# Moving the layer-norm gain rows from VectorE to GpSimd in a fused encoder layer, with two small steps of ScalarE and VectorE put in another place

## The chip, the cores and the metric

The kernel runs on one core of one Trainium2 chip. Its time is the device time in microseconds (us). Engines are named PE (TensorE), ACT (ScalarE), DVE (VectorE), POOL (GpSimd) and SP (the engine that issues most DMAs).

## The reference, cut to what matters

One encoder layer over two sequences (512 and 1024 rows of width 1024, 12 tiles of 128 rows in all). After a token mixer (stage one) and before a mixture of experts (stage three), this is computed per row:

```python
mod = silu(c) @ w_ada + b_ada            # one row per sequence: sh1, sc1, g1, sh2, sc2, g2
mix = token_mixer(...) @ w_out           # [A|B] W_out
x = layer_norm(ALPHA * x + g1 * mix, ln1_g, ln1_b)
h = x * (1 + sc2) + sh2                  # goes to the router and to the experts
logits = h @ [w_route_group | w_route_expert]
```

The kernel folds the modulation of h into the norm. With `rstd` and the negative mean `m` of a row's residual r, `h = (r + m) * G * rstd + B`, where `G = (1 + sc2) * ln1_g` and `B = sh2 + (1 + sc2) * ln1_b`. G and B depend on the sequence q alone (q = 0 for tiles 0 to 3, q = 1 for tiles 4 to 11), and are kept as 128x1024 rows, the same in every partition. Here they are called the gain rows.

## The kernel before, in words

Each engine has its own instruction list, written by hand; engines meet at semaphores alone, and an engine never passes a wait. The stage that the change touches follows stage one (the token mixer over six pairs of tiles) and runs once over the 12 tiles t. Every fp32 product with weights is done as three matmuls on a high and a low part (`three`).

PE, for each tile t from 2 on: `mix_half(t, 0)` (24 matmuls of 512 columns), then `route(t - 2)` (the router's 8 products; in tile 2 it is `h2_transposes(0)` instead), every second tile a small `rank` or `pick`, then `mix_half(t, 1)` (24 more), in tile 2 also `route(0)`, then `h2_transposes(t - 1)`. Its waits: `route(t)` waits for `h2T_copied` (ACT has copied tile t's transposes to SBUF) and for `logit_read` (DVE has taken the logits of tile t - 1 out of the one bank that they share); `mix_half(t, 0)` waits for DVE's low part of z (`z2_l_made`) and for the residual of tile t - 2.

DVE, for each tile: `second(t)` (gate the mix by g1, two reads of PSUM; add ALPHA x; the mean), `low_z(t + 2)`, `h2_out(t)` (the variance, then two SCALAR_TENSOR_TENSOR instructions: (r + m) * G, and * rstd + B), `x1_out(t)` (the same two with ln1_g and ln1_b), `logits_out(t - 1)`, and then `select` (even tiles: the top experts) or `places` and `picks` (odd tiles). `h2_out(t)` writes a single buffer h2, so that it waits until PE has transposed the tile before.

ACT, for each tile: `high_z(t + 2)`, which waits until PE has made the whole mix of tile t, `copy_h2T(t - 1)`, and `square(t)`, from which DVE's variance comes. In tile 2 `copy_h2T(0)` stands ahead of `high_z(4)`.

POOL does `rstd_of(t)` for each tile, one power of one column, and nothing else in this stage. It hands rstd back to `h2_out(t)`.

The gain rows are made in place by DVE, three instructions of 128x1024 for each q: `gain_first(q)` (two) and `gain_last(q)` (one). For q = 0 the first two stand ahead of stage one's last steps `gate_u(5)` and `b_out(5)`, the third behind them. For q = 1 all three stand between tiles 1 and 2. Both wait for `mod2_loaded`, DMAs that SP issues: ln1_g, ln1_b, g1, sc2, sh2 for q = 0 (80 in all), and three more for q = 1 (128).

After the stage PE, DVE and POOL finish the lists of rows for each expert, and the experts' loop (stage three) runs to the last stage.

Of the kernel before, what the change touches and what calls it, by code (L numbers as in the profile page):

```python
# [26 lines left out]
ALU = mybir.AluOpType  # L27
# [8 lines left out]
SEQ_TILES = ((0, SEQS[0] // P), (SEQS[0] // P, NT))  # L36
# [73 lines left out]
def encoder(nc, ins, outs):  # L110
    ctx = ExitStack()
    with ctx:
# [129 lines left out]
        sc2b = r.take("sc2b", [P, D])  # L242
        sh2b = Region(PB0).take("sh2b", [P, D])
# [8 lines left out]
        g1b, sc2b, sh2b = [[halves(b), w_col[:, 2 * j + 2:2 * j + 4, 1, :]] for j, b in enumerate((g1b, sc2b, sh2b))]  # L252
        ln_g2, ln_b2 = halves(ln_g), halves(ln_b)
        gain_tmp, squares1 = w_mid[:, 4:6, 1, :], w_mid[:, 6:8, 1, :]
# [108 lines left out]
        def bcast(row, n):  # L363
# [10 lines left out]
        S = {n: sem(n) for n in (  # L374

            "c_loaded rows_loaded small_loaded sp_rows_loaded wsp_loaded ident_made c_silu cT_made c_ready c_low mod_init"
            " colsT_made cols_ready wspT_made wspT_ready rowsum_made rowsum_ready off_made off_ready"
            " edge_iota spl_ones"

            " x_loaded xT_made x0_ready ada_h_made ada_l_made ada_made mod_hl_made mod_cols mod_made"  # L380
            " k_mod k_high k_low win_h_made win_l_made h_ready hT_h_made hT_l_made"
            " late_h_made late_l_made late_made late_row added_h added_l g2_loaded g2_made g2_row g2_added"
# [5 lines left out]
            " res_ready var_ready rstd_ready shift_ready x1_ready x1_stored h2_ready h2_stored h2T_made h2T_copied"  # L388
            " logit_made logit_read"

            " rt_consts sel_ready ranked rank_read pick_ready picked tab_ready eid_ready list_pe list_dve w_act"

            " idx_ready gathered xgT_made xT_h_made xT_l_made gu_split_h gu_split_l dn_split_h"
            " dn_split_l gu_used dn_used silu_made act_ready aT_e_made aT_h_made aT_l_made y_ready"
# [264 lines left out]
        def _(pool):  # L659
# [60 lines left out]
            def rstd_of(t):  # L720
                pool.wait_ge(S["var_ready"], t + 1)
                nc.gpsimd.tensor_tensor(rstd[:], mv[:, 1:2], half_neg[:], ALU.pow).then_inc(S["rstd_ready"], 1)  # L722

            for t in range(NT):
                rstd_of(t)

            pool.wait_ge(S["tab_ready"], 1)
            pool.wait_ge(S["h2_stored"], 16 * NT)
# [50 lines left out]
        def _(act):  # L779
# [160 lines left out]
            def copy_h2T(t):  # L940

                act.wait_ge(S["h2T_made"], t + 1)
                if t >= 1:
                    act.wait_ge(S["logit_made"], t)
                for b in range(2):
                    last = nc.scalar.activation(h2T[:, 4 * b:4 * b + 4, :], ps[4 + b][:].rearrange("p (k m) -> p k m", k=4), ACT.Copy)
                last.then_inc(S["h2T_copied"], 1)

            for t in range(NT):
                if t == NT - 4:  # L950
                    act.wait_ge(S["a_ready"], NP)
                    act.wait_ge(S["b_copied"], NP)
                    act.wait_ge(S["fb_copied"], 2)
                if t == 2:
                    copy_h2T(0)
                if t < NT - 2:
                    high_z(t + 2, t % 2, t // 2 + 1)
                if t >= 2:
                    copy_h2T(t - 1)
                square(t)  # L960
            copy_h2T(NT - 1)
# [112 lines left out]
        def _(dve):  # L1074
            st = Steps(dve, S["dve_steps"], S["dve_carrier"])
            nv = nc.vector
# [212 lines left out]
                norm_v(2 * i)  # L1289
            low_wout(1)  # L1290
            norm_v(NT - 1)

            def gain_first(q):

                dve.wait_ge(S["mod2_loaded"], 16 * (5 + 3 * q))
                st.done(nv.scalar_tensor_tensor(gain_tmp, sc2b[q], 1.0, ln_b2, ALU.add, ALU.mult))
                st.done(nv.scalar_tensor_tensor(sc2b[q], sc2b[q], 1.0, ln_g2, ALU.add, ALU.mult))
                st.sync()

            def gain_last(q):  # L1300
                st.done(nv.tensor_tensor(sh2b[q], sh2b[q], gain_tmp, ALU.add))
                st.sync()

            gain_first(0)
            gate_u(NP - 1)
            b_out(NP - 1)
            gain_last(0)

            def second(t, q):

                dve.wait_ge(S["mix_made"], t + 1)
                if t >= 2:
                    dve.wait_ge(S["x1_stored"], 16 * (t - 1))
                for b in range(2):
                    st.done(nv.tensor_tensor(res[t % 2][:, b, :], ps[2 * (t % 2) + b][:], g1b[q][:, b, :], ALU.mult))
                st.sync()
                dve.wait_ge(S["xr_loaded"], 16 * (t + 1))
                nv.scalar_tensor_tensor(res[t % 2], halves(xr), ALPHA, res[t % 2], ALU.mult, ALU.add, accum_out=stat[:, 0:1]).then_inc(S["res_ready"], 1)
                dve.wait_ge(S["res_ready"], t + 1)
                nv.tensor_scalar(mv[:, 0:1], stat[:, 0:1], -1.0 / D, None, ALU.mult).then_inc(S["shift_ready"], 1)  # L1320

            def h2_out(t, q):
                dve.wait_ge(S["res_normed"], t + 1)
                nv.tensor_scalar(mv[:, 1:2], stat[:, 1:2], 1.0 / D, EPS, ALU.mult, ALU.add).then_inc(S["var_ready"], 1)
                dve.wait_ge(S["shift_ready"], t + 1)
                if t >= 1:
                    dve.wait_ge(S["h2_stored"], 16 * t)
                    dve.wait_ge(S["h2T_made"], t)
                st.done(nv.scalar_tensor_tensor(halves(h2), res[t % 2], mv[:, 0:1], sc2b[q], ALU.add, ALU.mult))
                dve.wait_ge(S["rstd_ready"], t + 1)  # L1330
                st.sync()
                nv.scalar_tensor_tensor(halves(h2), halves(h2), rstd[:, 0:1], sh2b[q], ALU.mult, ALU.add).then_inc(S["h2_ready"], 1)  # L1332
# [6 lines left out]
            def logits_out(t):  # L1339
                dve.wait_ge(S["logit_made"], t + 1)  # L1340
                nv.tensor_tensor(logits[:, t, :], ps[6][:, 0:NG + NE], router_b[:], ALU.add).then_inc(S["logit_read"], 1)
# [53 lines left out]
                                         ALU.is_equal, ALU.mult).then_inc(S["pick_ready"], 1)  # L1395

            dve.wait_ge(S["a_ready"], NP)

            for t in range(NT):
                q = 0 if t < SEQ_TILES[0][1] else 1  # L1400
                second(t, q)
                if t == 2:
                    logits_out(0)
                if t < NT - 2:
                    low_z(t + 2, t % 2, t // 2 + 1)
                else:
                    if t == NT - 1:
                        places(4)
                if t == 0:
                    edge_out(NP - 1, 6, 2)  # L1410
                    dve.wait_ge(S["rt_consts"], 10)
                h2_out(t, q)
                if t == NT - 1:
                    picks(4)
                x1_out(t)
                if t == 1:
                    gain_first(1)
                    gain_last(1)
                if t >= 2:
                    logits_out(t - 1)  # L1420
                    if t % 2 == 0:
                        select(t // 2 - 1)
                    elif t < NT - 1:
                        places((t - 3) // 2)
                        picks((t - 3) // 2)
# [546 lines left out]
```

## Time and profile before

| | us |
|---|---|
| median of 3 runs | 1327.22 (1326.94 to 1330.86) |
| time of the profiled execution | 1326.94 |
| its span in the profile | 1325.2 |
| busy: PE, DVE, ACT, POOL | 1225.8, 951.3, 643.6, 198.8 |
| mean granted TensorE clock | 0.967 of full speed |

The span is what lies between the first and the last instruction; the run's own time is 1.7 us longer. Times of day below ("at 359.82") count from the span's start. The stage in question lies between about 341 and 505 us. Matmuls are pipelined, so that a matmul record may begin before the one ahead of it has ended.

### The profile page before, as it was taken

The page shows a single profiled execution, that of the slowest core. Times are in us where ns is not written, and L with a number is a line of the kernel's source. Part 1 is how long each engine was busy: PE and PEld are TensorE (multiplying, and loading weights), DVE is VectorE, ACT ScalarE, POOL GpSimd, SP SyncE. Part 2 cuts the span into 40 slices and gives each one's busy share as a digit, 9 for nine tenths or more (in the row PEclk, how much of TensorE's full clock was granted, in tenths as well). Part 3 has the DMA queues.
Part 4 walks back from the last instruction along what each step waited for, and adds up shares of the span by engine and source line. Part 5 has one row for each costly group of instructions (what it writes and reads, how often), then busy time and mean ns, then how long its engine had stood idle before and what let it go on. Part 6 is the DMA issues. An engine that isn't in the chain of part 4 may idle for free.

```text
span 1325.2 us, 23169 instructions
## 1 busy us (share of the span) xinstructions
PE 1225.8 (93%) x6396; PEld 1009.1 (76%) x6397; DVE 951.3 (72%) x1203; ACT 643.6 (49%) x666; POOL 198.8 (15%) x242
## 2 busy tenths in 40 slices
PE   4989989999999997799999999999999999999490
PEld 4778879998888872688888888888888888888240
DVE  3666555457899987854788656664889988886197
ACT  4453321123221213564677545644777788775221
POOL 0001101000011011111122111111121222212022
PEclk8899989999999998899999999999999999999796
DMA  9743231015432457775999757775999999996983
GB/s 309 240 126 105 88 96 49 17 30 193 160 112 112 175 211 281 271 266 212 360 384 401 299 221 299 261 269 205 366 400 398 390 407 389 398 395 224 384 303 127
DMA packets 121645, 329.08 MB, mean 248 GB/s; under 512 B 12040, under 2 KB 43904, under 8 KB 121604
## 3 DMA queue, kind: packets, MB, share of 16 engines
q1 hardware_dynamic: 107412, 288.08, 58.4%
q0 software_dynamic: 12320, 34.15, 7.3%
q10 hardware_dynamic: 1872, 6.29, 1.2%
q8 instruction: 26, 0.43, 0.1%
q14 instruction: 15, 0.12, 0.0%
HBM read 296.97 MB, written 39.42 MB: 254 GB/s over the span
## 4 chain that ended last, share of the span: by engine, by line
PE 72%; DVE 17%; DMA 3%; issue 3%; ACT 2%; POOL 1%; SPq 0%; DVEq 0%; POOLq 0%; ACTq 0%
PE bank L1582 17%; PE bank L1584 17%; PE bank L1583 17%; PE bank L1595 3%; PE bank L1597 3%; PE bank L1596 3%; PE bank L1878 3%; POOL rstd L722 1%; PE bank L1902 1%; DVE h L1332 1%; DMA y_rows<-y_sb,s_idx 1%; DVE gu_l L1467 1%; DVE fin L1546 1%; DVE fin L1561 1%; DVE gated L1542 1%
## 5 line engine op out<-in xcount | busy, mean ns | idle before, releaser
L1467 DVE TENSOR_TENSOR gu_l<-gu_raw,gu_h (+1 forms) x128 | 287.3, 2285 | 40.7 <-ACT gu_h L966 26.9
L1582 PE MATMUL bank<-gu_h,xT_h 128*128 (+1 forms) x624 | 248.6, 398 | 6.3 <-DVE xT_l L1486 3.7
L1584 PE MATMUL bank<-gu_h,xT_l 128*128 (+1 forms) x624 | 244.7, 392 | 0.0
L966 ACT ACTIVATE gu_h<-gu_raw (+1 forms) x128 | 238.7, 1928 | 11.8 <-issue 11.6
L1583 PE MATMUL bank<-gu_l,xT_h 128*128 (+1 forms) x624 | 244.3, 392 | 0.0
L1471 DVE TENSOR_TENSOR dn_l<-dn_raw,dn_h (+1 forms) x64 | 143.6, 2285 | 5.9 <-issue 4.2
L1582 PEld LDWEIGHTS bank<-gu_h,xT_h 128*128 128x128 f32 x624 | 118.3, 190 | 30.3 <-DVE xT_l L1486 4.1
L1584 PEld LDWEIGHTS bank<-gu_h,xT_l 128*128 128x128 f32 x624 | 118.1, 189 | 25.3
L1583 PEld LDWEIGHTS bank<-gu_l,xT_h 128*128 128x128 f32 x624 | 118.5, 190 | 23.5
L1582 PE MATMUL bank<-dn_h,aT_h 128*128 (+1 forms) x312 | 124.8, 400 | 2.5 <-DVE aT_l L1481 2.5
L1584 PE MATMUL bank<-dn_h,aT_l 128*128 (+1 forms) x312 | 121.7, 390 | 0.0
L1583 PE MATMUL bank<-dn_l,aT_h 128*128 (+1 forms) x312 | 121.6, 390 | 0.0
L970 ACT ACTIVATE dn_h<-dn_raw (+1 forms) x64 | 119.1, 1914 | 1.7 <-DMA dn_raw<-in_w_down 1.6
L1595 PE MATMUL bank<-hT_h,win_h 128*128 128x256 f32 x384 | 111.3, 290 | 8.6 <-ACT z2T L865 4.4
L976 ACT ACTIVATE act_s<-bank 128x512 f32<-128x512 f32 x39 | 23.3, 598 | 182.9 <-PE bank L1584 182.9
L1597 PE MATMUL bank<-hT_h,win_l 128*128 128x256 f32 x384 | 108.9, 284 | 0.0
L1596 PE MATMUL bank<-hT_l,win_h 128*128 128x256 f32 x384 | 108.8, 283 | 0.0
L751 POOL DMA_INDIRECT y_rows<-y_sb,s_idx x39 | 72.1, 1849 | 194.1 <-ACT y_sb L996 194.1
L1477 DVE TENSOR_TENSOR act_a<-bank,act_s 128x512 f32<-128x512 f32 x39 | 27.0, 691 | 85.9 <-ACT act_s L976 85.9
L1595 PEld LDWEIGHTS bank<-hT_h,win_h 128*128 128x128 f32 x384 | 74.2, 193 | 11.1 <-DVE hT_l L1127 5.5
L1582 PE MATMUL bank<-wout_h,z_h 128*128 128x512 f32 x192 | 77.4, 403 | 0.0
L1584 PE MATMUL bank<-wout_h,z_l 128*128 128x512 f32 x192 | 75.9, 395 | 0.0
(275 smaller groups left out, 2118.1 us busy)
## 6 DMA issues: line engine op xcount, KB each, us to landing
gu_raw<-in_w_gate_up SPq DMA_DIRECT2D x128, 1024.0 KB, 7.6
dn_raw<-in_w_down SPq DMA_DIRECT2D x64, 1024.0 KB, 7.4
y<-y_rows SPq DMA_DIRECT2D x24, 512.0 KB, 5.0
ada_raw<-in_w_ada SPq DMA_DIRECT2D x20, 512.0 KB, 5.3
ada_raw<-in_w_ada SPq DMA_DIRECT2D x10, 1024.0 KB, 5.3
win_raw<-in_w_in SPq DMA_DIRECT2D x8, 768.0 KB, 7.5
h_rows<-h SPq DMA_DIRECT2D x12, 512.0 KB, 2.6
fin<-x_rows SPq DMA_DIRECT2D x12, 512.0 KB, 13.9
```

The source lines that it names most:

```text
L751: nc.gpsimd.indirect_dma_start(out=y_d, out_offset=bass.IndirectOffsetOnAxis(ap=s_idx[:, 0:1], axis=0), in_=y_sb[:], in_offset=None, bound ...
L966: nc.scalar.activation(gu_slot(gu_h, e, c), gu_slot(gu_raw, e, c), ACT.Copy).then_inc(S["gu_split_h"], 1)
L970: nc.scalar.activation(dn_slot(dn_h, e, c), dn_slot(dn_raw, e, c), ACT.Copy).then_inc(S["dn_split_h"], 1)
L1467: nv.tensor_tensor(gu_slot(gu_l, e, c), gu_slot(gu_raw, e, c), gu_slot(gu_h, e, c).bitcast(F32), ALU.subtract).then_inc(S["gu_split_l"], 1)
L1471: nv.tensor_tensor(dn_slot(dn_l, e, c), dn_slot(dn_raw, e, c), dn_slot(dn_h, e, c).bitcast(F32), ALU.subtract).then_inc(S["dn_split_l"], 1)
L1582: mm(out, lh, rh, start=start, stop=False)
L1583: mm(out, lh, rl, start=False, stop=False)
L1584: return mm(out, ll, rh, start=False, stop=stop)
L1595: mm(out, win_h[:, k, c], hT_h[s][:, k, :], start=start, stop=False)
L1596: mm(out, win_h[:, k, c], hT_l[s][:, k, :], start=False, stop=False)
L1597: return mm(out, win_l[:, k, c], hT_h[s][:, k, :], start=False, stop=stop)
L1878: last = nc.tensor.transpose(ps[2 + k // 4][:, (k % 4) * P:(k % 4 + 1) * P], xg[:, k * P:(k + 1) * P], ident[:])
```

## The change

Five edits, all around the gain rows:

1. POOL gets `gain_rows(q, part)`. Part 0 waits for `mod2_loaded`, makes sc2 + 1 in place and multiplies it by ln1_b into `gain_tmp`; part 1 adds `gain_tmp` to sh2 in place and multiplies sc2 + 1 by ln1_g in place. These are four instructions of 128x1024 for each q, where DVE had three. A new semaphore `gains_made` counts the finished q.
2. For q = 0 both parts stand ahead of POOL's first `rstd_of`; for q = 1 part 0 follows `rstd_of(1)` and part 1 follows `rstd_of(2)`.
3. DVE loses `gain_first` and `gain_last`. It waits for `gains_made` in each `h2_out`, and for `mod2_loaded` before the loop and again before tile 4.
4. ACT: in tile 2 `copy_h2T(0)` moves behind `high_z(4)`.
5. DVE: in tile 2 `logits_out(0)` moves from behind `second(2)` to behind `x1_out(2)`.

```diff
+            def gain_rows(q, part):
+                if part == 0:
+                    pool.wait_ge(S["mod2_loaded"], 16 * (5 + 3 * q))
+                    st.done(nc.gpsimd.tensor_scalar(sc2b[q], sc2b[q], 1.0, None, ALU.add))
+                    st.sync()
+                    st.done(nc.gpsimd.tensor_tensor(gain_tmp, sc2b[q], ln_b2, ALU.mult))
+                    st.sync()
+                else:
+                    st.done(nc.gpsimd.tensor_tensor(sh2b[q], sh2b[q], gain_tmp, ALU.add))
+                    nc.gpsimd.tensor_tensor(sc2b[q], sc2b[q], ln_g2, ALU.mult).then_inc(S["gains_made"], 1)
+                    st.sync()
+            gain_rows(0, 0)
+            gain_rows(0, 1)
             for t in range(NT):
                 rstd_of(t)
+                if t in (1, 2):
+                    gain_rows(1, t - 1)
...
-                if t == 2:
-                    copy_h2T(0)
                 if t < NT - 2:
                     high_z(t + 2, t % 2, t // 2 + 1)
                 if t >= 2:
+                    if t == 2:
+                        copy_h2T(0)
                     copy_h2T(t - 1)
                 square(t)
...
-            def gain_first(q):
-                dve.wait_ge(S["mod2_loaded"], 16 * (5 + 3 * q))
-                st.done(nv.scalar_tensor_tensor(gain_tmp, sc2b[q], 1.0, ln_b2, ALU.add, ALU.mult))
-                st.done(nv.scalar_tensor_tensor(sc2b[q], sc2b[q], 1.0, ln_g2, ALU.add, ALU.mult))
-                st.sync()
-            def gain_last(q):
-                st.done(nv.tensor_tensor(sh2b[q], sh2b[q], gain_tmp, ALU.add))
-                st.sync()
-            gain_first(0)
             gate_u(NP - 1)
             b_out(NP - 1)
-            gain_last(0)
...
                 dve.wait_ge(S["shift_ready"], t + 1)
+                dve.wait_ge(S["gains_made"], q + 1)
...
             dve.wait_ge(S["a_ready"], NP)
+            dve.wait_ge(S["mod2_loaded"], 16 * 5)
             for t in range(NT):
+                if t == SEQ_TILES[0][1]:
+                    dve.wait_ge(S["mod2_loaded"], 16 * 8)
                 second(t, q)
-                if t == 2:
-                    logits_out(0)
...
                 x1_out(t)
-                if t == 1:
-                    gain_first(1)
-                    gain_last(1)
                 if t >= 2:
+                    if t == 2:
+                        logits_out(0)
                     logits_out(t - 1)
```

## Rows read from the trace of the kernel before

**Rows 1.** Windows, stage 341 to 505: us, busy of PE, PEld, DVE, ACT, POOL, clock, DMA, GB/s.
```profile
341.00:505.00 164.00, 160.86 (x840) 131.84 (x839) 149.23 (x329) 38.83 (x59) 18.83 (x12) 1.00 0.44 162
```

**Rows 2.** Timeline of PE without the mix: start, us, line; waits in brackets.
```profile
353.36 1.03 PE L1775 MATMUL bank<-ident,h 128*128 128x128 f32 x8
...
359.82 1.87 PE L1797 MATMUL bank<-router_w,h2T 128*128 128x36 f32 x16
361.52 1.07 PE L1775 MATMUL bank<-ident,h 128*128 128x128 f32 x8
...
368.04 1.87 PE L1797 MATMUL bank<-router_w,h2T 128*128 128x36 f32 x16
...
490.78 1.03 PE L1775 MATMUL bank<-ident,h 128*128 128x128 f32 x8
```

**Rows 3.** Waits between 333 and 505: PE's longest, in total, times, longest.
```profile
PE bank L1797 <- DVE logits L1341: 2.0, 1, 2.0
```

**Rows 4.** Timeline of DVE: gain rows, tile 2, and the start of tile 11.
```profile
333.05 1.22 DVE L1296 SCALAR_TENSOR_TENSOR w_mid<-sc2b,ln_b 128x1024 f32<-128x1024 f32 x1 [7.35 <-DMA sh2b<-mod_rows]
...
360.10 1.22 DVE L1296 SCALAR_TENSOR_TENSOR w_mid<-w_col,ln_b 128x1024 f32<-128x1024 f32 x1
...
366.41 0.18 DVE L1341 TENSOR_TENSOR logits<-bank,router_b 128x36 f32<-128x36 f32 x1
...
367.80 0.15 DVE L1324 TENSOR_SCALAR mv<-stat 128x1 f32<-128x1 f32 x1
...
373.37 0.19 DVE L1341 TENSOR_TENSOR logits<-bank,router_b 128x36 f32<-128x36 f32 x1
...
492.04 1.29 DVE L1315 TENSOR_TENSOR res<-bank,w_col 128x512 f32<-128x512 f32 x2
```

**Rows 5.** Timeline of ACT, tiles 1 and 2.
```profile
354.43 1.09 ACT L946 ACTIVATE h2T<-bank 128x512 f32<-128x512 f32 x2
360.02 1.06 ACT L881 ACTIVATE z_h<-z2T 128x1024 fp32r<-128x1024 f32 x1 [4.50 <-PE bank L1584]
362.63 1.09 ACT L946 ACTIVATE h2T<-bank 128x512 f32<-128x512 f32 x2 [1.55 <-PE bank L1775]
366.53 1.15 ACT L938 ACTIVATE w_mid<-w_col,mv 128x1024 f32<-128x1024 f32 x1 [2.81 <-DVE mv L1320]
```

**Rows 6.** Timeline of POOL: a power alone and beside DVE, a copy beside DVE.
```profile
324.57 0.55 POOL L674 TENSOR_TENSOR v_rstd<-v_mv,half_neg 128x1 f32<-128x1 f32 x1 [6.21 <-DVE v_mv L1187]
...
354.78 1.57 POOL L722 TENSOR_TENSOR rstd<-mv,half_neg 128x1 f32<-128x1 f32 x1 [8.04 <-DVE mv L1324]
...
544.63 1.22 POOL L738 COPY g_idx<-table_g 128x1 int32 x1 [15.00 <-PE bank L1878]
```

**Rows 7.** Timeline of DVE beside those POOL instructions.
```profile
354.65 1.28 DVE L1329 SCALAR_TENSOR_TENSOR h<-res,mv,sc2b 128x1024 f32<-128x1024 f32 x1
...
541.32 6.69 DVE L1467 TENSOR_TENSOR gu_l<-gu_raw,gu_h  x3
```

**Rows 8.** Timeline of POOL: instructions of more than one column.
```profile
304.08 0.29 POOL L696 TENSOR_SCALAR_AFFINE_SELECT tri<-tri 128x128 f32<-128x128 f32 x1
304.35 0.44 POOL L701 IOTA iota_c<- 128x384 f32 x1
304.75 0.13 POOL L701 IOTA iota_p<- 128x1 f32 x1
```

**Rows 9.** Timeline of PE where it had been idle, start of the experts' loop.
```profile
548.66 1.12 PE L1902 MATMUL bank<-ident,act_a 128*128 128x128 f32 x4 [4.82 <-DVE act_a L1477]
552.31 0.79 PE L1582 MATMUL bank<-gu_h,xT_h 128*128 x1 [2.54 <-DVE gu_l L1467]
```

**Rows 10.** Windows of PE around them: us, busy, granted clock, DMA, GB/s.
```profile
548.00:550.00 2.00, 1.12 (x4) 0.67 0.29 37
550.00:552.00 2.00, 0.00 (x0) 0.50 0.62 229
...
554.00:556.00 2.00, 2.00 (x7) 0.63 0.00 0
```

More of the change, by code:

```diff
@@ L389, in encoder @@
             " logit_made logit_read"
-            " rt_consts sel_ready ranked rank_read pick_ready picked tab_ready eid_ready list_pe list_dve w_act"
+            " gains_made rt_consts sel_ready ranked rank_read pick_ready picked tab_ready eid_ready list_pe list_dve w_act"
             " idx_ready gathered xgT_made xT_h_made xT_l_made gu_split_h gu_split_l dn_split_h"
```

## The prediction

> **What bounds the kernel now.** I read the windows by stage first. Between 341 and 505 us PE is busy 160.86 of 164 us and DVE 149.23 [rows 1], so the busy shares alone leave it open which of the two sets the pace. The gain rows are DVE's work, so that this is the question on which everything hangs. The timeline of PE answers it: from the transposes at 353.36 to those at 490.78 [rows 2], and for 30 us ahead of them, no record of PE is preceded by a wait. Only behind that does the view of waits show one of 2.0 us for DVE's logits, in the last tile [rows 3]. PE, then, works without a break through 11 of the 12 tiles, and DVE follows it: the mix of tile 11 is done at about 490.9 (the transposes behind it start at 490.78 [rows 2]), and DVE takes it up at 492.04 [rows 4], 1.1 us later. DVE is nearly full as well, but it is the follower. Two things come out of this. Whatever DVE saves ahead of tile 11 can be worth no more than that 1.1 us. And whatever makes PE wait anywhere in that stretch is lost from the first tenth of a microsecond, but for the same 1.1 us: PE has no idle time in which to make it good. Behind tile 11 the chain of work runs through DVE, then the lists and the experts' loop, all of them started by the step before, so that a delay of DVE there reaches the end unchanged.
>
> **The gain rows leave DVE.** For q = 1 the reader sees the first of three instructions at 360.10, 1.22 us long [rows 4]; three of them are 3.7 us. For q = 0 it is the same 3.7 us, of which some 1.3 us come back because `gate_u(5)` still waits for PE. DVE so comes out up to 6.1 us ahead on its own count, but `h2_out(1)` can't write before PE's transposes at 353.36 are through, about 354.2 [rows 2], and before the change it wrote at 354.65 [rows 7]. The whole gain of q = 0 ends there, but for 0.4 us. What q = 1 saves ends at PE's next mix. I put the gain of edit 3 at the 1.1 us of slack in tile 11, and no more. Its new waits on DVE for the DMAs cost nothing: the first set has landed at 333.05, where DVE starts on it now [rows 4], and behind both waits stands work of 338 us and later.
>
> **Edit 4, the copy of ACT.** Before, `copy_h2T(0)` ran at 354.43 [rows 5] beside the mix, and `route(0)` started at 359.82 with no wait [rows 2]. Behind `high_z(4)` it has to wait for the mix of tile 2 to be complete: `high_z(4)` starts at 360.02, the next ACT instruction can start about 1.0 us later, and the two copies take 1.09 [rows 5], which gives 362.07. PE stands at `route(0)` from 359.82, and goes on at about 362.15. That is 2.3 us of idle PE, and all that follows on PE is 2.3 us later.
>
> **Edit 5, the logits of DVE.** `route(1)` started at 368.04 [rows 2], after the logits of tile 0 had been read at 366.41 [rows 4]. The new place is just ahead of the read that was at 373.37 [rows 4]. When is that reached now? The transposes of tile 1 move from 361.52 [rows 2] to 363.85, and the copies behind them from 362.63 [rows 5] to 364.96, ending at 366.05. `square(2)` stands behind those copies on ACT, so it starts at 366.0 instead of 366.53 [rows 5], however early DVE is ready. From there to the variance it was 1.27 us (366.53 [rows 5] to 367.80 [rows 4]), and from the variance to the logits slot 5.57 us (to 373.37 [rows 4]). That gives 367.27 and 372.84, and with 0.19 us for the read and a little for the semaphore PE may start `route(1)` at 373.1. It would have been there at 368.04 + 2.33 = 370.37. Edits 4 and 5 together make PE 373.1 - 368.04 = 5.1 us late. Queued behind `route(1)` is all the rest of the mix, and DVE waits for that.
>
> **The POOL instructions.** No row shows one of 128x1024. An IOTA goes from 0.13 us for 1 column to 0.44 for 384, 0.8 ns a column; AFFINE_SELECT, which reads one input, takes 0.29 for 128, 1.3 ns a column above the same 0.13 [rows 8]. At 1024 columns that is 1.0 us at the least (an instruction with no input), 1.4 with one input, 1.9 with two if a second read adds what the first one added (0.5 ns), and 2.8 if it doubles the column. I take 2.2 us, between the last two, as these have two inputs; ends 1.0 and 2.8. For q = 0 the four instructions start at 333.05 and need some 8 us, up to 341.5, while the first `h2_out` reads them at about 342.5, and even a start as late as 347 would vanish at the transposes of tile 0. For q = 1 nobody waits for `gains_made` until tile 4. So by their own length they cost nothing.
>
> What they cost by standing beside DVE is another matter. A power of one column takes 0.55 us when DVE is idle [rows 6], and 1.57 when it starts at 354.78, in the middle of DVE's instruction of 354.65 to 355.93 [rows 7]: it ends 0.4 us after that one. The copy at 544.63 took 1.22 us instead of about 0.2 and ended at 545.85 [rows 6]; DVE's run of three started at 541.32 [rows 7], 2.2 us each, so its second one ended at 545.75. POOL, then, stays out while a DVE instruction with two SBUF inputs runs, and gets in at the seam between two of them. If only one of the two can have whatever it is, then DVE stays out while POOL has it, and a POOL instruction here has it for 2.2 us, not for one column. That mirror is an assumption: no POOL instruction of before is long enough to show it. Where does it hurt? Part 0 of q = 1 runs beside `h2_out(1)` and `x1_out(1)`, and may push `second(2)` from 359.9 to 361.5 or 363.5; `square(2)` is held to 366.0 by ACT's copies anyway, so that is covered to the last tenths. Part 1 of q = 1 starts with the end of `rstd_of(2)` at 369.1, and the three DVE instructions between it and the logits of tile 0 (the second of `h2_out(2)`, both of `x1_out(2)`) all have two SBUF inputs. POOL's two instructions get in at two of the seams, and each holds DVE for 2.2 us: 4.4 us, on the very path that edit 5 made PE wait for. `route(1)` then starts at 377.5. The bounds are 0 (DVE isn't held) and 2 x 2.8 = 5.6 us.
>
> The Trainium skill states the mirror: SBUF — State Buffer, section Who interferes with whom, says that a DVE instruction with two SBUF inputs and a GpSimd instruction that reads SBUF exclude each other for the whole instruction, and that whoever issues first has it. The trace agrees with the half that it shows, 1.57 us against 0.55. GPSIMD Engine Reference, section 3.1, has 4497 ns for a two-input instruction of 2048 columns; an estimate from it for 1024 is 2.3 us, and the sum by it would be 0.2 us higher.
>
> **The clock of PE.** In that case PE stands still from 370.4 to 377.5, 7 us. In this trace PE was idle for 4.82 us up to 548.66, and the granted clock fell from full (2.4 GHz) to half (1.2 GHz), 0.67 in the window of 548 to 550 and 0.50 behind it; PE started again at 552.31 and had half the clock until about 555.5 (0.63 over 554 to 556) [rows 9, 10]. That is 3.2 us of work at half speed, a loss of 1.6 us. The 2.0 us wait of the last tile [rows 3] didn't bring it down. I take 1.6 us, ends 0 and 3.2, should the clock fall at both waits.
>
> **The sum.** PE late by 5.1 (edits 4 and 5), 4.4 (POOL holds DVE) and 1.6 (clock) is 11.1 us; minus the 1.1 us that DVE was behind it in tile 11 makes 10.0. On the profiled execution's 1326.94 us, which lies 0.28 under the median of the runs, this gives 1336.9; I say 1337.0, 0.7% slower.
>
> **The rivals.**
> - POOL holds DVE, but the clock stays full: 10.0 - 1.6 = 8.4, so 1335.3. For it: one wait of 2.0 us did nothing to the clock. Against: 7 us is longer than the idle time that did.
> - The orders alone: DVE isn't held, or for a part only. Then 5.1 - 1.1 = 4.0, so 1331.0 (up to 1334 when held in part). For it: DVE's instructions are as long beside a one-column POOL instruction as without one (1.28 us at 354.65 [rows 7]). Against: that such a hold would last too short to be seen.
> - POOL's instructions take longer than I can bound, or the clock falls at both waits: 5.1 + 5.6 + 3.2 - 1.1 = 12.8 and above, 1339.7 and more.
> - PE's order waits don't appear, since its records hide slack of some microseconds (their ends are modelled) and it could take `route` later: then only the 1.1 us of slack counts, 1326, no change. Against: eight transposes and the 24 matmuls behind them take 6.5 us in tile 2 (361.52 to 368.04 [rows 2]) and the same 6.5 in every tile after it, which work with slack in it would not.
> - The other side: DVE, not PE, sets the pace. The place would be the hand-over of the residuals to `mix_half(t, 0)`; saved are 3.7 us for q = 1 and up to 2.4 for q = 0, so 1320.8. It decides only if PE's idle time before tile 11 were above 0, and if `route(1)` found its logits before 368; the trace has neither.
>
> **How the numbers follow.** POOL holds DVE and the clock falls: 0.40. It holds and the clock stays: 0.20. The orders alone or in part: 0.22. 1339.7 and more: 0.06. No change: 0.06. Faster: 0.06. About 0.3% (4 us) is what a measurement of this kernel tells from no change; the orders alone, at 4.0, lie on that line, and 0.05 of their 0.22 goes to "within". Faster 0.06, within 0.11, slower 0.83. The range must hold the first three cases with their bounds and may leave out 2 in 10: from 1330.5 (the orders alone, a little less) to 1341.0 (2.8 us for each POOL instruction, 3.2 for the clock, and something for the runs' own spread). For the likeliest case by itself, 1335.5 to 1339.5.
>
> **What would show it.** In the profile of the changed kernel: no gain-row lines on DVE, eight POOL instructions of 128x1024, about 2.2 us each when alone; a wait of PE of about 2.3 us at `route(0)` for ACT's h2T, and one of 2.7 us (orders alone) or 7 us (held) at `route(1)` for DVE's logits; DVE instructions in `h2_out(2)` and `x1_out(2)` of some 3.5 us or with gaps of 2.2 us where they had 1.28; a window under full clock around 377 us; from tile 3 on DVE waiting for the mix in every tile, and the mix of tile 11 done at about 502. The prediction is wrong if PE finds `h2T` or the logits ready at those two places, if those DVE instructions keep 1.28 us, or if a POOL instruction takes 4 us or more.

## The result and the profile after

The changed kernel is slower: 1341.84 us median of 4 runs (1341.69 to 1345.88) against 1328.45 of the kernel before (4 runs, 1326.94 to 1330.86), a ratio of 1.0106 (95% interval 1.0081 to 1.0133). That is 13.4 us where 10.0 were predicted, and 0.84 us above the range. The changed kernel's profiled execution took 1342.34 us, with a span of 1340.6 and a mean granted clock of 0.961.

One thing first, for all comparisons of times of day below. In the profile after, everything at the start of the stage is 2.27 us earlier than before: the transposes of tile 0 start at 351.09, and stood at 353.36 [rows 2]. Stage one's length varies from one execution to the next: over the 13 profiles of this document those transposes start between 351.09 and 353.66, in kernels of both kinds. So 2.27 is added to a time of after when it is set beside one of before.

Timeline of PE in the profile after (start, us, line, operation; waits in brackets), without the mix:

```profile
359.93 1.95 PE L1801 MATMUL bank<-router_w,h2T 128*128 128x36 f32 x16 [2.21 <-ACT h2T L963]
...
376.25 3.60 PE L1801 MATMUL bank<-router_w,h2T 128*128 128x36 f32 x16 [6.30 <-DVE logits L1345]
...
386.71 1.03 PE L1779 MATMUL bank<-ident,h 128*128 128x128 f32 x8
...
502.07 1.04 PE L1779 MATMUL bank<-ident,h 128*128 128x128 f32 x8
...
507.55 7.70 PE L1826 MATMUL bank<-g_raw,c_cols 128*2 128x512 f32 x12
...
539.26 1.97 PE L1882 MATMUL bank<-ident,xg 128*128 128x128 f32 x8 [6.05 <-DMA xg<-h_rows,g_idx]
```

Both waits that were predicted are there, `route(0)` at 359.93 (362.20 on before's count, 362.15 predicted) and `route(1)` at 376.25 (378.52; 377.5 predicted), where before had none [rows 2]. The transposes of tile 2, at 386.71 here, stand in the timeline of PE before as

```profile
375.42 1.03 PE L1775 MATMUL bank<-ident,h 128*128 128x128 f32 x8
```

so that from there on PE is 13.56 us late (386.71 + 2.27 - 375.42), and it is still 13.56 us late at those of tile 10 (502.07 against 490.78 [rows 2]). So the whole loss of the stage is made in tiles 2 and 3, and nothing is won or lost in the eight tiles after them. The last two rows are in the tail, and will matter below.

Windows of PE in the same profile (us, busy, granted clock, DMA share, GB/s): two long stretches, then single ones.

```profile
357.56:502.07 144.51, 136.00 (x698) 0.95 0.37 135
502.07:543.79 41.72, 29.77 (x114) 0.83 0.75 288
362.00:364.00 2.00, 2.00 (x11) 0.55 0.54 217
364.00:366.00 2.00, 2.00 (x7) 0.60 0.37 86
...
372.00:374.00 2.00, 0.00 (x0) 0.61 0.64 262
374.00:382.00 8.00, 5.75 (x22) 0.50 0.17 66
382.00:384.00 2.00, 2.00 (x9) 0.83 0.00 0
...
506.00:512.00 6.00, 6.00 (x14) 0.50 1.03 419
```

The first stretch, from where `route(0)` once stood to the transposes of tile 10, took 130.96 us before (359.82 to 490.78 [rows 2], at full clock); now it takes 144.51, 13.55 more. The second, up to the same point of the experts' loop, took 38.17 and now takes 41.72, 3.55 more. The clock is at its lower level, 1.2 GHz, after the wait of 2.21 us too, then again after the 6.30, and a third time at 506 to 512.

Timeline of DVE in the same profile, from the last step of stage one to tile 2:

```profile
333.66 3.11 DVE L1219 TENSOR_TENSOR z2T<-gated_s,z2T 128x1024 f32<-128x1024 f32 x1
...
339.33 3.13 DVE L1321 SCALAR_TENSOR_TENSOR w_col<-xr,w_col 128x1024 f32<-128x1024 f32 x1
...
353.83 1.29 DVE L1333 SCALAR_TENSOR_TENSOR h<-res,mv,sc2b 128x1024 f32<-128x1024 f32 x1
355.56 2.06 DVE L1336 SCALAR_TENSOR_TENSOR h<-h,rstd,sh2b 128x1024 f32<-128x1024 f32 x1 [0.44 <-POOL rstd L722]
...
358.85 3.25 DVE L1341 SCALAR_TENSOR_TENSOR res<-res,rstd,ln_b 128x1024 f32<-128x1024 f32 x1
...
367.99 3.41 DVE L1336 SCALAR_TENSOR_TENSOR h<-h,rstd,sh2b 128x1024 f32<-128x1024 f32 x1 [0.46 <-POOL rstd L722]
371.32 3.36 DVE L1339 SCALAR_TENSOR_TENSOR w_col<-w_col,mv,ln_g 128x1024 f32<-128x1024 f32 x1
374.71 1.28 DVE L1341 SCALAR_TENSOR_TENSOR w_col<-w_col,rstd,ln_b 128x1024 f32<-128x1024 f32 x1
375.92 0.19 DVE L1345 TENSOR_TENSOR logits<-bank,router_b 128x36 f32<-128x36 f32 x1
```

and of POOL and ACT in the same stretches:

```profile
330.42 2.79 POOL L728 TENSOR_SCALAR sc2b<-sc2b 128x1024 f32<-128x1024 f32 x1 [7.56 <-DMA sh2b<-mod_rows]
333.29 2.40 POOL L730 TENSOR_TENSOR w_mid<-sc2b,ln_b 128x1024 f32<-128x1024 f32 x1
335.77 3.27 POOL L733 TENSOR_TENSOR sh2b<-sh2b,w_mid 128x1024 f32<-128x1024 f32 x1
339.00 2.37 POOL L734 TENSOR_TENSOR sc2b<-sc2b,ln_g 128x1024 f32<-128x1024 f32 x1
...
355.50 2.77 POOL L728 TENSOR_SCALAR w_col<-w_col 128x1024 f32<-128x1024 f32 x1
358.36 2.66 POOL L730 TENSOR_TENSOR w_mid<-w_col,ln_b 128x1024 f32<-128x1024 f32 x1
...
367.93 2.39 POOL L733 TENSOR_TENSOR w_col<-w_col,w_mid 128x1024 f32<-128x1024 f32 x1
370.28 3.32 POOL L734 TENSOR_TENSOR w_col<-w_col,ln_g 128x1024 f32<-128x1024 f32 x1
```

```profile
364.79 1.15 ACT L955 ACTIVATE w_mid<-w_col,mv 128x1024 f32<-128x1024 f32 x1 [0.47 <-DVE mv L1323]
```

Two DVE instructions of tile 2 that had 1.28 us [rows 7] have 3.41 and 3.36, and the two engines take turns: POOL's first runs from 367.93 to 370.32, and DVE's record, begun at 367.99, closes 1.1 us after that, at 371.40; POOL's second lasts from 370.28 to 373.60, stretched by a wait of its own, and DVE's closes again 1.1 us later, at 374.68. Added up, DVE's two are 4.2 us longer, which is the hold that was put at 4.4. In tile 1 two of them are longer by 0.78 and 1.97 us.

The gain rows of q = 0 do the same, where the prediction had no such cost. DVE's instructions at 333.66 and 339.33 were these before:

```profile
337.14 1.22 DVE L1202 TENSOR_TENSOR z2T<-gated_s,z2T 128x1024 f32<-128x1024 f32 x1
...
342.18 1.23 DVE L1318 SCALAR_TENSOR_TENSOR w_col<-xr,w_col 128x1024 f32<-128x1024 f32 x1
```

They are 1.89 and 1.90 us longer beside POOL's at 333.29 to 339.00. So DVE isn't ahead when it comes to `h2_out(1)`, but behind: 353.83 is 356.10 on before's count, against 354.65 [rows 7]. The one instruction of ACT shows what reaches tile 2: `square(2)` now waits 0.47 us for DVE, and starts at 364.79 (367.06 on before's count, 366.0 predicted).

### The profile page after: what moved, and what is told of

Read it like the earlier page. It is cut to its first block, busy times and chain, and to the rows that moved or that the text cites. A ratio compares the mean times of both kernels' runs of the same rounds, so it can differ in the third digit from the quotient of the medians.

```text
span 1340.6 us, 23186 instructions
## 1 busy us (share of the span) xinstructions
PE 1231.7 (92%) x6396; PEld 1014.8 (76%) x6397; DVE 956.2 (71%) x1197; ACT 642.9 (48%) x666; POOL 216.1 (16%) x250
## 4 chain that ended last, share of the span: by engine, by line
PE 81%; DVE 9%; DMA 4%; issue 2%; ACT 2%; SPq 0%; POOL 0%; DVEq 0%; POOLq 0%; ACTq 0%
PE bank L1586 20%; PE bank L1588 19%; PE bank L1587 19%; PE bank L1599 3%; PE bank L1601 3%; PE bank L1600 3%; PE bank L1882 3%; PE bank L1801 2%; PE bank L1906 1%; DMA y_rows<-y_sb,s_idx 1%; DVE fin L1550 1%; DVE fin L1565 1%; DVE gated L1546 1%; PE bank L1593 1%; DVE gu_l L1471 1%
## 5 line engine op out<-in xcount | busy, mean ns | idle before, releaser
L1599 PEld LDWEIGHTS bank<-hT_h,win_h 128*128 128x128 f32 x384 | 73.9, 192 | 11.1 <-DVE hT_l L1144 5.5
```

The source lines that it names most:

```text
L1599: mm(out, win_h[:, k, c], hT_h[s][:, k, :], start=start, stop=False)
```

## The experiments

### Which edit makes PE wait

`e1_orders_only` is the kernel before with edits 4 and 5, the gain rows left on DVE:

```diff
-                if t == 2:
-                    copy_h2T(0)
                 if t < NT - 2:
                     high_z(t + 2, t % 2, t // 2 + 1)
                 if t >= 2:
+                    if t == 2:
+                        copy_h2T(0)
...
-                if t == 2:
-                    logits_out(0)
...
                 if t >= 2:
+                    if t == 2:
+                        logits_out(0)
                     logits_out(t - 1)
```

> The kernel before with edits 4 and 5 alone (ACT's copy behind high_z(4), DVE's logits of tile 0 behind x1_out(2)); the gain rows stay on DVE. Theory (orders, hold and clock add up): PE waits 2.3 us at route(0) and about 3 us at route(1), whose start comes 5.5 us later than before (373.37 - 0.1 for the logits slot, against 368.04); no DVE instruction is stretched. Minus 1.1 us of slack this makes +4.4 us, and up to 5 more where the clock falls again behind tile 11: 4 to 9 us slower than before, against 13 to 15 for the whole change. Rival (the POOL instructions alone make the loss, the orders are covered): within 1 us of before and no wait at the two routes.

`e2_gains_only` is the changed kernel with these two edits undone, so that only the gain rows move.

> The changed kernel with edits 4 and 5 undone: the gain rows on POOL, the orders as before. Theory: PE finds h2T and the logits at both routes; DVE's instructions beside POOL's are stretched by the same 2.8 us in tile 1 and 4.2 us in tile 2, together more than the 3.7 us that DVE saves there, so that DVE starts tile 3 about 4.7 us later than before. DVE has no idle time either and keeps that to tile 11: 4 to 5 us slower than before, with PE waiting at transposes of tile 3 and later for h2. Rival one (PE alone sets the pace, DVE's loss is absorbed): within 1 us of before. Rival two (the orders are harmless, POOL does it all): 13 to 15 us slower.

`e3_copy_only` is the kernel before with edit 4 alone (the first half of that diff), `e4_logits_only` with edit 5 alone (the second).

> The kernel before with edit 4 alone. Theory: PE waits 2.2 us at route(0) and none at route(1); the clock falls for about 3 us behind the wait, which costs another 1.5. Minus the 1.1 us of slack: 2 to 3 us slower. Rival (the clock doesn't fall at so short a wait by itself): 1.1 us slower. Rival (PE can absorb it): 0.

> The kernel before with edit 5 alone. Theory: no wait at route(0), 5.4 us of waiting at route(1), whose start is again at 373.5 against 368.04. One long wait instead of two short ones lets the clock fall once, at the long one, which costs 1.6 to 3.2: 6 to 8 us slower, more than both edits together if these keep the clock up. Rival (each order costs its own and they add): 4.4 minus the 1.2 of the copy, about 3 us slower.

| | median, us (range) | ratio to before (95%) |
|---|---|---|
| before (14 runs, beside the next four) | 1329.76 | 1 |
| edits 4 and 5 | 1337.69 (1337.13 to 1338.32) | 1.0062 (1.0045 to 1.0079) |
| gain rows alone | 1335.59 (1333.87 to 1338.11) | 1.0044 (1.0029 to 1.0058) |
| edit 4 alone | 1332.2 (1331.15 to 1334.05) | 1.0022 (1.0013 to 1.0032) |
| edit 5 alone | 1337.91 (1336.02 to 1340.18) | 1.0062 (1.0044 to 1.008) |
| the whole change again (before beside it: 13 runs, 1329.76) | 1344.26 (1342.47 to 1345.12) | 1.011 (1.0093 to 1.0127) |

Every part costs time, as expected, and the parts don't add. Edit 5 alone costs as much as edits 4 and 5 together (8.2 and 7.9 us), since both end in the one wait at `route(1)`, which takes in what edit 4 had cost. PE in the two of them, edits 4 and 5 together first (its wait at `route(0)` is 2.21 us, as in the whole change), then edit 5 alone:

```profile
373.06 2.55 PE L1797 MATMUL bank<-router_w,h2T 128*128 128x36 f32 x16 [1.39 <-DVE logits L1341]
...
383.65 1.04 PE L1775 MATMUL bank<-ident,h 128*128 128x128 f32 x8
```

```profile
373.32 3.60 PE L1797 MATMUL bank<-router_w,h2T 128*128 128x36 f32 x16 [5.04 <-DVE logits L1341]
...
384.99 1.04 PE L1775 MATMUL bank<-ident,h 128*128 128x128 f32 x8
```

Counted again from the transposes of tile 0 (352.81 and 353.44 in these two), `route(1)` starts 5.6 and 5.2 us later than at 368.04 [rows 2] (5.1 predicted). But the transposes of tile 2, which come 7.38 us behind `route(1)` before (375.42 to 368.04), are 10.6 and 11.7 us behind it, and PE has no wait in between. The 3.2 and 4.3 us above 7.38 are what the lower clock costs, not 1.6.

Edit 4 alone isolates the short wait, and this is the case that tells most about the clock. Its PE, and the windows of the granted clock:

```profile
360.43 1.95 PE L1797 MATMUL bank<-router_w,h2T 128*128 128x36 f32 x16 [2.21 <-ACT h2T L946]
...
370.29 1.87 PE L1797 MATMUL bank<-router_w,h2T 128*128 128x36 f32 x16
```

```profile
362.00:364.00 2.00, 2.00 (x14) 0.71 0.03 8
364.00:366.00 2.00, 2.00 (x6) 0.50 0.48 123
```

From `route(0)` to `route(1)` it takes 9.86 us, 8.22 before (368.04 - 359.82 [rows 2]): 1.64 us go to the clock, after a wait of 2.21 us, with no other wait. By its median the edit costs 2.4 us, by its ratio 2.9 (2 to 3 expected).

The gain rows alone keep both `route` steps free of waits, and yet cost 5.8 us (4 to 5 expected). The row that shows where is not in the prediction:

```profile
393.29 1.06 PE L1779 MATMUL bank<-ident,h 128*128 128x128 f32 x8 [3.77 <-DVE pos L1380]
```

PE's transposes of tile 3 wait 3.77 us until DVE has read the ranks out of the bank that both use, its first step in working out the places. DVE takes up the mix of tile 3 at 383.13, 30.23 us behind the transposes of tile 0 (352.90), and did so 25.00 us behind them before (378.36 and 353.36): it is 5.2 us late. Moving the gain rows hasn't freed DVE, then, but the reverse. It lost 1.8 us up to tile 1 and was held for 2.8 and 4.3 us in tiles 1 and 2, against 3.7 us of work less. In the whole change this wait doesn't appear, as `route(1)` has made PE late by then.

### Is it POOL's reading that holds DVE?

`e5_part1_later` is the changed kernel with part 1 of q = 1 one tile later, where nobody waits for DVE:

```diff
-                if t in (1, 2):
-                    gain_rows(1, t - 1)
+                if t in (1, 3):
+                    gain_rows(1, t // 2)
```

> The changed kernel with part 1 of POOL's gain rows for q = 1 one tile later, behind rstd_of(3). Theory (POOL's two instructions hold DVE on the path to the logits of tile 0): the two stretched DVE instructions move to tile 3, those of tile 2 are back at 1.28 us, and route(1) starts 4.2 us earlier than in the changed kernel, with a wait of about 2 us in place of 6.3. In tile 3 the same 4.2 us fall beside the mix and are for the most part covered. In all 2 to 4 us faster than the changed kernel. Rival (the wait at route(1) comes from the new order alone, whatever POOL does): the wait stays at 6 us and the time within 1 us of the changed kernel's.

`e6_writes_in_tile2` and `e10_reads_in_tile2` add to it two instructions of POOL of 1024 columns in the old place, into the half of `w_mid` that nothing uses here: the first only writes, the second reads and writes.

```diff
+                if t == 2:
+                    for n in (0, 2):
+                        st.done(pool.memset(w_mid[:, n:n + 2, 1, :], 0.5))              # e6
+                        st.done(nc.gpsimd.tensor_copy(w_mid[:, n:n + 2, 1, :], ln_b2))  # e10
+                    st.sync()
```

> As e5, but with two extra POOL instructions behind rstd_of(2) that write 1024 columns each of an unused tile and read nothing. Theory: what DVE and POOL exclude each other for is the reading; these take about 1 us each and leave DVE's instructions of tile 2 at 1.28 us; the time is e5's. Rival (any POOL instruction on SBUF holds DVE): two DVE instructions of tile 2 are longer by about 1 us each, and route(1) starts 2 us later than in e5.

> As e5, but with two extra POOL copies of 1024 columns (one input each) into an unused tile behind rstd_of(2). Theory: they read, so they hold DVE as the two-input ones did, each for its own length, which I put at 1.0 to 1.4 us; route(1) starts 2 to 3 us later than in e5. Rival (only two-input POOL instructions hold DVE): DVE's instructions of tile 2 stay at 1.28 us.

With part 1 moved away, the kernel takes 1340.4 us (1338.86 to 1341.95; before was 1331.06 beside it), ratio 1.007 (1.0049 to 1.0091), against 1.0106 (1.0081 to 1.0133) and 1.011 (1.0093 to 1.0127) for the whole change; it lies clear of the second only. The trace is plainer. DVE's two instructions in tile 2 are back at 1.29 and 1.28 us, and PE waits 2.42 us at `route(1)` instead of 6.30, at 374.92, which is 3.9 us earlier when both are counted from the transposes of tile 0. The two others had one run each, 1340.4 (writes) and 1344.48 (reads); their rows say more than these. DVE and POOL with the writes, then with the reads:

```profile
369.64 1.28 DVE L1340 SCALAR_TENSOR_TENSOR h<-h,rstd,sh2b 128x1024 f32<-128x1024 f32 x1 [0.46 <-POOL rstd L722]
...
369.56 1.84 POOL L743 MEMSET w_mid<- 128x1024 f32 x2
```

```profile
370.79 2.05 DVE L1340 SCALAR_TENSOR_TENSOR h<-h,rstd,sh2b 128x1024 f32<-128x1024 f32 x1 [0.46 <-POOL rstd L722]
372.76 2.05 DVE L1343 SCALAR_TENSOR_TENSOR w_col<-w_col,mv,ln_g 128x1024 f32<-128x1024 f32 x1
...
370.71 3.03 POOL L743 COPY w_mid<-ln_b 128x1024 f32<-128x1024 f32 x2
```

Two fills of 0.92 us each start beside DVE's instruction, and it keeps its 1.28. Two copies of 1.5 us make two DVE instructions 0.77 us longer each, and `route(1)` comes 1.4 us later than in e5; a hold of each copy's own length, 2 to 3 us in all, had been expected. So an instruction of POOL that reads SBUF holds a two-input instruction of DVE, and one that only writes doesn't. How long it holds is another matter. POOL's two-input instructions of 2.4 us held DVE for 1.9 to 2.1 us each, nearly their whole length, but the copies for half of theirs, and the `sc2 + 1` of part 0 (355.50, one input) for 0.78 us of its 2.77. The Trainium skill (SBUF — State Buffer, Who interferes with whom) gives the exclusion for instructions that read, and these rows agree with that; a hold of the whole instruction, which the prediction took from there, they show for two inputs only.

### What the clock costs

`e7_pe_filled` is the changed kernel with unused matmuls ahead of the two waits, into a bank that nobody reads at that time, so that PE isn't idle for long:

```diff
+            def keep_busy(n):
+                for _ in range(n):
+                    mm(ps[7][:], wout_h[:, 0, 0, 0:P], wout_h[:, 1, 0, :], start=True, stop=True)
...
+                    if t == 3:
+                        keep_busy(26)
                     route(t - 2)
...
+                    keep_busy(9)
                     route(0)
```

> The changed kernel with matmuls on PE that nobody uses, put ahead of the two waits: 9 ahead of route(0) and 26 ahead of route(1), 2.1 and 6.1 us at full clock, so that PE isn't idle while it waits. Theory (half the clock behind the two waits costs 3 us): the granted clock stays at full from 359 to 390 us, route(1) starts when it did, and the mix of tile 3 ends 3.2 us earlier than in the changed kernel; the time is 3 us shorter, or more if the clock doesn't fall behind tile 11 either. Rival (the clock isn't part of it, or the fillers cost what they save): within 1 us of the changed kernel, or slower.

```profile
377.57 1.95 PE L1801 MATMUL bank<-router_w,h2T 128*128 128x36 f32 x16 [2.06 <-DVE logits L1345]
...
385.03 1.03 PE L1779 MATMUL bank<-ident,h 128*128 128x128 f32 x8
```

The granted clock is full from 354 to 392, and from `route(1)` to the transposes of tile 2 it is 7.46 us, as before (7.38) and 3.0 less than in the changed kernel (386.71 - 376.25 = 10.46). Those 3.0 us are shown in the trace. In the time, where 3 us less were expected, they are not settled: the profiled executions are 1339.56 here and 1342.47 in the second profile of the changed kernel (see below), but the medians are 1343.2 (1339.56 to 1344.95, ratio 1.0099, 1.0079 to 1.0119) and 1341.84 and 1344.26.

### The tail

Behind the transposes of tile 10 the changed kernel lost 3.55 us more, where the prediction had it gain 1.1. The changed kernel ran again to see which of that stays.

> The changed kernel once more, beside e8 and e9, so that they have it on the same chip. It should be 13 to 15 us slower than before; in its profile PE waits about 6 us for the rows gathered first (L1882), as in the first profile.

In that second profile the 12 matmuls of `g2_part` (the row of g2, which the last stage needs) ahead of the transposes of tile 11 run at full clock, 5.31 us as before. In the first profile they took 7.70. From the transposes of tile 10 to the gather of the first expert's rows it is 28.61 us before, 30.23 in the first profile after and 27.54 in the second. Without the fall of the clock, then, the tail is 1.07 us shorter than before: most of it is the slack of tile 11 (DVE takes up the mix 0.42 us behind those transposes, 1.26 before; 1.1 predicted for the whole). With the fall, 2.7 us longer.

What stays in both is the wait for the gather. Here are the issue of the gather, the issue of the four loads of w_down and the start of the transposes that need the gathered rows, of the kernel before and then of the changed one:

```profile
519.39 1.12 POOL L741 DMA_INDIRECT xg<-h_rows,g_idx  x1 [0.92 <-POOL g_idx L738]
...
521.75 10.16 SPq L595 DMA_DIRECT2D dn_raw<-in_w_down  x4
...
523.98 1.26 PE L1878 MATMUL bank<-ident,xg 128*128 128x128 f32 x8 [1.96 <-DMA xg<-h_rows,g_idx]
```

```profile
532.30 1.13 POOL L758 DMA_INDIRECT xg<-h_rows,g_idx  x1 [0.92 <-POOL g_idx L755]
...
532.95 9.34 SPq L595 DMA_DIRECT2D dn_raw<-in_w_down  x4
```

Before, in its profile, the gather had 2.36 us to itself, and PE could start 4.59 us after its issue. In the changed kernel the 4 MB are issued 0.65 us behind it, and it is 6.96 us. The loads wait for `g2_made`, the end of those `g2_part` matmuls; before they ran at half clock just there (4.43 us for the last six, 2.74 after) and so came later. So the kernel before was spared in its profiled execution. `e8_dn_behind_gather` (changed kernel) and `e9_before_dn_behind_gather` (kernel before) put the loads behind the gather:

```diff
             sp.wait_ge(S["g2_made"], 1)
+            sp.wait_ge(S["gathered"], 16)
             for n in range(DN_SLOTS):
                 load_dn(n // 2, n % 2)
```

> The changed kernel with one more wait on SP: the four loads of w_down issue when the first gather of rows has landed. Theory (the gather, issued at 532.3, shares the DMA engines with those loads, issued at 532.95, and lands 2.4 us later for it than in the profile of before, where they were issued 2.4 us behind it): PE's wait for xg falls from 6.05 to about 3.6 us, and the time by 1.5 to 2.5 us. Rival (the gather is slow by itself, or the later loads cost as much): no change within 1 us.

> The kernel before with that same wait on SP. Theory: the profile of before was a run in which the gather came first (PE waited 1.96 us for xg); in runs where the list is ready with PE at full clock the loads come 0.65 us behind the gather, as in all the other profiles. Then this is 0 to 2 us faster than before. Rival: no effect at all, or slower since the w_down loads start later.

PE's wait in e8, then in e9:

```profile
535.54 1.97 PE L1883 MATMUL bank<-ident,xg 128*128 128x128 f32 x8 [3.55 <-DMA xg<-h_rows,g_idx]
```

```profile
522.70 1.09 PE L1879 MATMUL bank<-ident,xg 128*128 128x128 f32 x8 [3.78 <-DMA xg<-h_rows,g_idx]
```

The wait, 5.97 to 6.25 us in the profiles of all other kernels but before, falls to 3.55 (from the issue of the gather at 531.07 to PE it is 4.47 us). The changed kernel takes 1341.7 us with it (1339.53 to 1342.69), ratio 1.0091 (1.0074 to 1.0108), 2.6 us less than the 1344.26 beside it, though the intervals of the two overlap. The kernel before takes 1325.9 (10 runs, 1324.58 to 1330.16) against 1329.76, ratio 0.9974 (0.9965 to 0.9984): this is faster than both kernels, and by more than expected (0 to 2 us). That it gains 3.9 us in the time, while the profiled execution of before waits for the gather less than it does, says that most executions of before have this collision and the profiled one, the fastest of all 38 that were timed, had not. This last is inferred from the times; there is a trace of one execution of before only. And the gather alone can't be all of it: it is 2.2 to 2.5 us faster with the loads behind it (4.70 us in e9, 6.9 to 7.2 in every profile with the loads 0.65 us behind it). Where the rest of the 3.9 us comes from is open.

## Why the prediction was wrong

The direction and the mechanism at `route(1)` were right, and the likeliest case was the one that came. The size was short by 4.84 us (1341.84 - 1337.0): the term for the clock was half of what it is, the gain rows of q = 0 were put at nothing, and the base was one lucky execution. Point by point:

- **What bounds the kernel.** Right. PE, with no idle time before tile 11: every microsecond lost at `route(1)` was still missing, to the hundredth, at tile 10. And the slack of DVE behind it was worth 1.07 us (1.1 said).
- **Edit 4.** Right in its place and size: 2.21 us of wait, `route(0)` 2.38 us late (2.33 said).
- **Edit 5.** Right in the main: `route(1)` 5.6 and 5.2 us late with no instruction of DVE held (5.1 said). The 0.4 us between the two are the first fall of the clock, which the sum of the orders had left out (see the next point but one).
- **POOL holds DVE.** Right: 4.2 us (4.4 said), gone when part 1 moves by a tile. The mirror that was an assumption is shown by the copies and the fills.
- **The gain rows of q = 0, put at nothing.** Wrong. Of them the prediction said that "even a start as late as 347 would vanish at the transposes of tile 0", and it looked at their own length alone. It used the hold by POOL, which it knew, for q = 1 only. Here q = 0 held DVE for 3.8 us (1.89 + 1.90), while it saved 1.2 us ahead of `gate_u(5)` and 1.2 behind it. So `h2_out(1)` began at 356.10 on before's count, and not at 354.2.
- **Part 0 of q = 1, "covered to the last tenths".** Wrong, but by its start and not by its own hold. The two instructions held DVE for 0.78 and 1.97 us, together less than the 3.6 us at the most (363.5 - 359.9) that were allowed for. Yet `second(2)` came at 362.02 (364.29 on before's count), since `h2_out(1)` had begun 1.9 us later than said. And the copies of ACT that were to cover it ended late too. The e1 kernel shows that part, as DVE isn't held in it:

```profile
365.88 1.15 ACT L938 ACTIVATE w_mid<-w_col,mv 128x1024 f32<-128x1024 f32 x1
```

  This is its `square(2)`, 13.07 us behind the transposes of tile 0 with no wait for DVE, where 12.64 were said (366.0 - 353.36): the transposes of tile 1 ran at the lower clock, and the copies follow them. In the whole change it is 13.70 (364.79 - 351.09). So `square(2)`, which starts all of tile 2's second half, is 1.06 us later than said, 0.43 by the clock and 0.63 by DVE. That makes `route(1)` 10.48 us late, not 9.46.
- **"a loss of 1.6 us" for the clock.** This is the step that failed most: 3.1 us (10.46 - 7.38). The fall that it went by had PE back for 3.2 us of work at half clock; here PE had the lower level from within the wait up to some 382.4, 6 us of work. The 6 us stood in the trace of before as well. There PE came back at 528.95, after a wait of 3.72 us, and worked at half clock up to 535 (window of PE, as above):

```profile
529.00:535.00 6.00, 6.00 (x14) 0.50 0.88 306
```

  So the term rested on the shorter of two cases that were there to read. Nor was the 2.0 us wait of the last tile a sign that short waits are free: one of 2.21 us cost 1.64 alone. In the whole change this first fall cost little of its own, because PE had to wait at `route(1)` anyway. With e1 and e4 the same term is 3.2 and 4.3 us. PE's lateness at tile 3 thus is 10.48 + 3.08 = 13.56, where 9.5 + 1.6 = 11.1 was said.
- **"a delay of DVE there reaches the end unchanged".** Not so. The tail changes with how PE and the loads meet in it: up to 2.7 us for a third fall of the clock, behind a wait of 1.17 us that before has too, and 2.4 us for the gather (6.96 - 4.59), both against the one profiled execution of before.
- **The base.** The sum stood on 1326.94, the fastest of before's executions. The median of before beside the change is 1328.45, 1.5 us more.

So the 4.84 us are 1.5 for the base, 1.0 for the later start of tile 2's second half, 1.5 for the clock, and 0.8 that the tail and the spread of the medians share, and which these runs don't separate. Against the profiled execution alone the sum nearly closes: the spans differ by 15.4 us, and with the 2.27 us of the earlier start 17.7; 10.0 + 1.0 + 1.5 + 2.7 + 2.4 is 17.6. Part of that is luck: from PE's transposes of the gathered rows to the first expert's matmuls 0.4 us were won, and 0.6 us were lost behind them, which no term names.

Of the rivals, the full clock, the orders alone and no change fall with the profile after. "DVE sets the pace" would have had the kernel faster by what DVE saves, and this was not put to the test, since DVE saved nothing: it came to tile 3 5.2 us late with the gain rows alone. Against it stand the rows of before, in which PE doesn't wait in this stage ahead of tile 11 [rows 2]. What the prediction did not have is the wait that a late DVE causes, PE's for the ranks in tile 3.

## What to carry to other kernels

Before work is moved to GpSimd, look at what VectorE does beside it: here instructions with two inputs on both engines took turns, so that the moved work was still paid by VectorE, and was paid where it stood. Ask this of every moved instruction, also of those that seem to have time enough; the four of q = 0 were passed over here. Put them beside a stretch where nobody waits for VectorE. When PE is the bound and never idle, price each new wait on it as its length plus the work it then does at the lower clock, which here cost from 1.6 to 4.3 us for waits of 1.4 to 6.6. And when a prediction is made from one profiled execution, read the tail for things that could fall differently in another one, such as a gather that happens to run ahead of a batch of loads.

## What the runs showed of the hardware

- On GpSimd, a 128x1024 fp32 instruction with one input (add a constant) took 2.77 to 2.80 us in all eight profiles that have it, more than one with two inputs (2.37 to 2.40 where it wasn't stretched), a copy about 1.5, and a fill 0.92. The Trainium skill (GPSIMD Engine Reference, section 4.1) has one-input work at roughly line rate and two-input work about twice as slow as on VectorE; the two-input row fits that (DVE's multiply-add took 1.28), the one-input row doesn't.
- A fill of GpSimd doesn't hold a two-input instruction of VectorE; a copy of 1.5 us holds it for 0.77, an added constant of 2.77 us for 0.78, an instruction with two inputs of 2.4 us for 1.9 to 2.2.
- The granted clock fell to half behind a wait of 2.21 us in all eight profiles that have that wait with no filling. In the tail, behind a wait of 1.17 to 1.52 us, it fell in four profiles (the changed kernel's first, e1, e4 and e10: `g2_part` took 6.5 to 7.7 us) and not in the other nine (5.3).
- A gather of 128 rows issued 0.65 us ahead of 4 MB of loads let PE start 6.9 to 7.2 us after its issue; with those loads 2.36 us later, or behind it, 4.5 to 4.7 us.
